# The second layer's values as two blocks of seven products, computed ahead of its pairs of heads

## The reference, cut to what matters

```python
h = jnp.einsum('bsd,de->bse', x, w_in[layer])            # 512 x 2048 times 2048 x 8192
qa, ka, va, ga, qb, kb, vb, gb = jnp.split(h, splits, axis=-1)   # eight of width 1024
ya = _dilated_attention(heads(qa, 16), heads(ka, 16), heads(va, 16), t5_bias)
yb = _neighbourhood_attention(heads(qb, 16), heads(kb, 16), heads(vb, 16), na_rpb[layer])
ya = merge(ya) * jax.nn.silu(ga.astype(jnp.float32))
yb = merge(yb) * jax.nn.silu(gb.astype(jnp.float32))
out = jnp.einsum('bse,ed->bsd', jnp.concatenate([ya, yb], -1), w_out[layer])
x = _layer_norm(DEEPNORM_ALPHA * x + out, ln_gain[layer], ln_bias[layer])
```

## Time and profile before

| | |
|---|---|
| median of three runs | 2478.79 us |
| the profiled execution, first to last instruction | 2477.0 us |
| PE busy | 2464.3 us (99%), 13712 matmuls |
| DVE busy | 1506.1 us (61%) |
| ACT busy | 841.0 us (34%) |
| POOL busy | 696.6 us (28%) |
| end of the first layer's products | about 1500 us |
| end of the pair steps | about 2310 us |

### The profile page before, as it was taken

The page is one execution under the profiler, slowest core; times in us unless marked ns, Lnnn a source line. Parts: engine busy times, 40 slices in busy tenths (PEclk is TensorE's granted clock), DMA queues, the critical chain, the costliest instruction groups (busy, mean ns, idle before and its releaser), DMA issues.

```text
span 2477.0 us, 36169 instructions
## 1 busy us (share of the span) xinstructions
PE 2464.3 (99%) x13712; PEld 2092.3 (84%) x13712; DVE 1506.1 (61%) x2529; ACT 841.0 (34%) x1281; POOL 696.6 (28%) x867
## 2 busy tenths in 40 slices
PE   9999999999999999999999999999999999999998
PEld 7788899999988888888888888888888888888887
DVE  5664877898779976655554333556465545455525
ACT  7422444544454333333222222223232322223221
POOL 0312455666512222232001220211122334343100
PEclk9999999999999999999999999999999999999999
DMA  7748333433456766777544444676656555546622
GB/s 287 223 162 271 114 126 128 130 135 136 137 173 211 259 230 237 241 244 274 178 165 149 136 153 128 205 196 205 205 176 212 172 175 160 171 153 214 242 96 102
DMA packets 102405, 452.53 MB, mean 183 GB/s; under 512 B 18006, under 2 KB 18006, under 8 KB 74182
## 3 DMA queue, kind: packets, MB, share of 16 engines
q1 hardware_dynamic: 38712, 241.58, 28.7%
q0 software_dynamic: 63568, 209.25, 26.8%
HBM read 351.47 MB, written 100.79 MB: 183 GB/s over the span
## 4 chain that ended last, share of the span: by engine, by line
PE 98%; DMA 1%; SPq 0%; DVE 0%; ACT 0%; issue 0%; DVEq 0%
PE bank L456 23%; PE bank L457 22%; PE bank L458 22%; PE bank L874 16%; PE bank L1258 5%; PE bank L1181 2%; PE bank L1319 2%; PE bank L1160 2%; PE bank L1043 1%; PE bank L1018 1%; DMA w_raw<-wst 1%; PE bank L955 1%; PE bank L1038 0%; PE bank L1008 0%; PE bank L898 0%; PE bank L713 0%
## 5 line engine op out<-in xcount | busy, mean ns | idle before, releaser
L445 DVE TENSOR_TENSOR w_lo<-w_raw,w_hi 128x2048 fp32r<-128x2048 f32 x164 | 375.9, 2292 | 369.5 <-ACT w_hi L440 367.3
L456 PE MATMUL bank<-act_b,w_hi 128*128 128x512 f32 x1280 | 501.6, 392 | 0.0
L457 PE MATMUL bank<-act_b,w_lo 128*128 128x512 f32 x1280 | 498.4, 389 | 0.0
L458 PE MATMUL bank<-act_b,w_hi 128*128 128x512 f32 x1280 | 498.1, 389 | 0.0
L440 ACT ACTIVATE w_hi<-w_raw 128x2048 fp32r<-128x2048 f32 x163 | 311.7, 1913 | 509.6 <-PE bank L458 435.9
L456 PE MATMUL bank<-act_a,w_hi 128*128 128x512 f32 (+1 forms) x1032 | 405.8, 393 | 0.0
L457 PE MATMUL bank<-act_a,w_lo 128*128 128x512 f32 (+1 forms) x1032 | 401.9, 389 | 0.0
L458 PE MATMUL bank<-act_a,w_hi 128*128 128x512 f32 (+1 forms) x1032 | 401.8, 389 | 0.0
L456 PEld LDWEIGHTS bank<-act_b,w_hi 128*128 128x128 f32 x1280 | 240.2, 188 | 54.5 <-issue 5.2
L458 PEld LDWEIGHTS bank<-act_b,w_hi 128*128 128x128 f32 x1280 | 240.3, 188 | 50.4
L457 PEld LDWEIGHTS bank<-act_b,w_lo 128*128 128x128 f32 x1280 | 240.3, 188 | 48.8
(11 more groups left out here) (376 smaller groups left out, 3351.7 us busy)
## 6 DMA issues: line engine op xcount, KB each, us to landing
w_raw<-wst SPq DMA_DIRECT2D x210, 1024.0 KB, 5.0
prob_t<-flip_d POOLq DMA_DIRECT2D x64, 512.0 KB, 4.8
flip_d<-flip POOLq DMA_DIRECT2D x56, 512.0 KB, 4.3
mix_d<-stage POOLq DMA_DIRECT2D x24, 512.0 KB, 3.2
mixg<-mix_d POOLq DMA_DIRECT2D x8, 1536.0 KB, 6.8
prob_tk<-flip_d POOLq DMA_DIRECT2D x32, 256.0 KB, 6.0
flip_d<-flip_a POOLq DMA_DIRECT2D x16, 512.0 KB, 2.9
b<-rows_2d POOLq DMA_DIRECT2D x16, 448.0 KB, 10.3
```

Source lines behind the costliest of these rows:

```text
L445: dve.tensor_tensor(w_lo[s][:], w_raw[s][:], w_hi[s][:].bitcast(F32), ALU.subtract).then_inc(lo_ready, 1)
L456: pe.matmul(out_ap, l_hi, r_hi, start=start, stop=False)
L457: pe.matmul(out_ap, l_lo, r_hi, start=False, stop=False)
L458: return pe.matmul(out_ap, l_hi, r_lo, start=False, stop=stop)
```

## The change

1. *Value stage.* Between the end of `wo_group` and pair step 0 stands a stage of 32 chunks (`value_chunk(n)`), which computes all 2048 value columns, token-major: tokens on the partitions, 512 columns in a bank. It consists of two blocks (`sg` 0 and 1, 1024 columns each). A block is a 2x2 split of tokens (256 each), inner dimension (1024 each) and columns (512 each), with seven products instead of eight (Strassen's scheme in Winograd's form): three in its first half (`ph` 0), four in its second, each over k = 0 to 7. The weights of a block are streamed in both halves, since four of the products use sums of weight blocks: chunks of 1536 columns in the first half and 2048 in the second.
2. *Sums of weights.* POOL makes them (`value_sums`), one per chunk in the first half and three in the second. ACT and DVE split each of the three or four parts on its own (`value_hi`, `value_lo`, 512 columns each). The sums have one buffer each, the split parts two.
3. *Sums of tokens.* Four sums of quarters of x1 are made once, from x1 in DRAM: all 16 tiles of x1 are now stored plainly to `x1_d` and loaded in quarters in the middle of the first half of block 0; two are DVE's (`s1_sum`, `s2_sum`), two POOL's (`s3_sum`, `s4_sum`), each in two pieces of 1024 columns, and each piece is split by ACT and DVE (`tokens_hi`, `tokens_lo`).
4. *Results.* DVE, ACT and POOL combine the seven products (`keep`, `first_block_out`, `u2_out` and so on), POOL stores them in 16 transfers per block to `v2_d`, which now holds all values.
5. *Pairs.* The pairs' weights hold queries, keys and gates only, cut as chunks of 1536, 1536, 1024 and 2048 columns (`PAIR_COLS`): 36, 36, 24 and 48 matmuls. Queries and keys are read after chunk 2, the gate after chunk 3, in a bank of its own (7). `v_to_tokens` is one load per dense pair (six per window pair). The 32 x 32 transposes and the four small stores go. On DVE the order in a beat changes: in beat 1 the split stands between `soft2_a` of tile 2 and of tile 3, and `queries_keys` between the flips. `beat` on PE is not changed.

The number of weight chunks goes from 216 to 248. The core of the diff:

```diff
+            def value_chunk(n):
+                sg, ph, k = v_phase(n)
+                operands = ((act_b, k, 0), (act_b, k + 8, 0), (s1_x, k, 0)) if ph == 0 else \
+                           ((s4_x, k, 0), (s3_x, k, 0), (s2_x, k, 0), (act_b, k + 8, 256))
+                order = V_ORDER[ph]
+                for pos, i in enumerate(order):
+                    if i + 1 < len(order):
+                        pe.wait_ge(vp_lo, VL0 + parts_before(n) + i + 1)
+                    else:
+                        pe.wait_ge(lo_ready, 2 * G_V + n + 1)
...
+                    act, row, c0 = operands[i]
+                    for t in range(2):
+                        for m, (l, r) in enumerate(((0, 0), (1, 0), (0, 1))):
+                            last = pe.matmul(v_bank(sg, ph, i, t), act[l][:, row, c0 + P * t:c0 + P * t + P], v_w[n % 2][i][r][:],
+                                             start=(k == 0 and m == 0), stop=(k == 7 and m == 2))
+                    last.then_inc(vp_used if pos + 1 < len(order) else chunk_used, 1)
```

```diff
+            def value_sums(n):
+                sg, ph, k = v_phase(n)
+                c = 2 * G_V + n
+                b11, b12, b21, b22 = (v_block(n, i) for i in range(4))
+                t1, t3, t2, t4 = v_sum
+                pool.wait_ge(w_loaded[n % 2], 8 * (c - n % 2) - 16)
+                jobs = ((t1, b12, b11, ALU.subtract),) if ph == 0 else \
+                       ((t3, b22, b12, ALU.subtract), (t2, t3[:], b11, ALU.add), (t4, t2[:], b21, ALU.subtract))
+                for i, (dst, l, r, op) in enumerate(jobs):
+                    if n:
+                        if ph == 0 or i == 2 or k == 0:
+                            pool.wait_ge(lo_ready, c)
+                        else:
+                            pool.wait_ge(vp_lo, VL0 + parts_before(n - 1) + i + 2)
...
+                    pool.tensor_tensor(dst[:], l, r, op).then_inc(vp_sum, 1)
```

```diff
+            # DVE, from chunk 3 to chunk 11 of the stage
+            value_lo(4, range(2))
+            s1_sum(1)
+            s2_sum(0)
+            tokens_lo(2, s1_x, s1_raw, 1)
+            value_lo(4, range(2, 3))
+            s2_sum(1)
+            value_lo(5)
+            tokens_lo(3, s3_x, s3_raw, 0)
+            value_lo(6)
+            tokens_lo(4, s2_x, s2_raw, 0, 2)
+            tokens_lo(5, s4_x, s4_raw, 0)
+            value_lo(7)
+            value_lo(8)
+            tokens_lo(6, s3_x, s3_raw, 1)
+            first_block_out(0)
```

```diff
             def pair_step(step, par, kind, before, gemm=True):
                 for cc in range(4):
                     if kind and cc % 2 == 0:
                         beat(kind, before, step, cc // 2, par)
...
-                    chunk_ready(pe, 2 * g + cc % 2)
-                    rows_t(pe, cc % 2, range(6), act_b, in2_banks(kind, cc))
...
+                    chunk_ready(pe, 4 * step + (2 * G_IN2 + cc))
+                    if cc < 3:
+                        for kt in range(PAIR_COLS[cc] // GC):
+                            k = 6 * cc + kt
+                            for n in range(2):
+                                last = mm3(pe, bank[n][:], wt(w_hi[cc % 2], kt, n * P, P), wt(w_lo[cc % 2], kt, n * P, P),
+                                           act_b[0][:, k, :], act_b[1][:, k, :], start=(k == 0), stop=(k == KT - 1))
```

More of the change, by code:

```diff
@@ new lines, in pair_step @@
+                    if cc < 3:
[5 more added lines that the diff above has]
+                    else:
+                        if not kind:
+                            pe.wait_ge(v_dve, VD0 + 20)
+                        else:
+                            pe.wait_ge(ev_act, evac_act(step - 1, 1))
+                            pe.wait_ge(ev_dve, evac_dve(step - 1, 1))
+                        for k in range(KT):
+                            last = mm3(pe, bank[GATE_BANK][:], wt(w_hi[1], k, 0, P, P), wt(w_lo[1], k, 0, P, P),
+                                       act_b[0][:, k, :], act_b[1][:, k, :], start=(k == 0), stop=(k == KT - 1))
+                            if k == CK - 1:
+                                last.then_inc(gate_half, 1)
@@ new lines, in _ @@
+            hi2(G_WO + 6)
+            x1_hi(3, 0)
+            split_hi(act, 2 * G_WO + 15, 1)
+            value_hi(0)
+            tokens_hi(s1_x, s1_raw, 0, 1, 0)
+            value_hi(1)
+            x1_hi(3, 1)
+            for n in range(2, 4):
+                value_hi(n)
+            value_hi(4, range(2))
+            tokens_hi(s1_x, s1_raw, 1, 2, 0)
+            value_hi(4, range(2, 3))
+            value_hi(5)
+            tokens_hi(s3_x, s3_raw, 0, 2, 1)
+            value_hi(6)
+            tokens_hi(s2_x, s2_raw, 0, 3, 1)
@@ L1704, in exp2 @@
+            keep(1, 1, v_p5, 2)
+            value_hi(25, range(2, 4))
+            for n in range(26, 32):
+                value_hi(n)
+            split_hi(act, 2 * G_IN2, 0, cols=PAIR_COLS[0])
             def exp2(kind, step, cc):
@@ new lines, in _ @@
+            split_lo(dve, 2 * G_WO + 15, 1)
+            value_lo(0)
+            s1_sum(0)
+            tokens_lo(1, s1_x, s1_raw, 0)
+            value_lo(1)
+            x1_out_of(3, 1, last=True)
+            for n in range(2, 4):
+                value_lo(n)
+            value_lo(4, range(2))
[6 more added lines that the diff above has]
+            tokens_lo(3, s3_x, s3_raw, 0)
@@ L2462, in soft2_a @@
+            value_lo(17)
+            third_block_out(0)
+            for n in range(18, 25):
+                value_lo(n)
+            first_block_out(1)
+            for n in range(25, 32):
+                value_lo(n)
+            split_lo(dve, 2 * G_IN2, 0, cols=PAIR_COLS[0])
+            u2_out(1)
+            u3_out(1)
+            second_block_out(1)
+            third_block_out(1)
             def soft2_a(kind, step, cc, par):
@@ new lines, in v_store @@
+            def v_store(src, row, col, done):
+                pool.wait_ge(*done)
+                for j in range(4):
+                    if col < 1024:
+                        at, step, block = 8 * row + j, 16, 4
+                    else:
+                        at, step, block = 256 * (j % 2) + 4 * row + j // 2, 8, 2
+                    pool.dma_start(bass.AP(v2_d, at * D + col, [[step * D, 32], [block * D, 2], [1, 512]]),
+                                   src[32 * j:32 * j + 32, :, :]).then_inc(v2_stored, 16)
@@ new lines, in _ @@
+            value_sums(2)
+            for s in range(2):
+                pool.wait_ge(x1_out[s], 464)
+            tokens_load(x_22, 12, 1, 1)
+            tokens_load(x_12, 12, 0, 3)
+            value_sums(3)
+            value_sums(4)
+            s3_sum(0)
+            value_sums(5)
+            s4_sum(0)
+            s3_sum(1)
+            value_sums(6)
+            s4_sum(1)
+            for n in range(7, 10):
+                value_sums(n)
+            v_store(v_u, 0, 0, (v_dve, VD0 + 2))
```

524 lines of the change are left out of this document (377 added, 147 removed).

## The result

The changed kernel takes 2540.3 us (median of 4 runs, 2539.2 to 2540.7) beside 2479.0 for the one before: 1.0249 times as long, 95% interval 1.0234 to 1.0264. The profiled execution's span is 2538.8 us. The forecast was slower, 2490 us, range 2463 to 2507: the sign is right, and the time lies outside the range.

The account below looks back on a forecast made before the run. TensorE's product count times their 0.227 us distance, plus its waits, was taken as the bound: 2477.0 - 21.8 + 31 (values' stage) + 2 (dense pairs) = 2488.2, plus 1.8 for the runs' median: 2490 us, range 2463 to 2507.

Parts of the forecast that it names:

- What bounds the kernel, and the 96 products: Whole kernel: TensorE's products, 0.227 us apart, set the time; 96 fewer products save 21.8 us.
- The values' stage, 31 us: New stage before the pairs: VectorE and GpSimd alternate on SBUF and stall TensorE by 31 us, bounds 0 to 45.
- 13, 8, 4 and 6: Values' stage: forecast stalls in us for first and second half of block one, then of block two.
- low parts read 1.7 us: Values' stage: sign that VectorE's 512-column low parts would read 1.7 us where GpSimd sums run.
- The dense pairs, 2 us with bounds 0 to 24: Dense pair steps: shorter half steps leave 0.8 us of cover for the second probabilities load, costing 2 us over 8 steps.
- load that is late by 2 us beside the bias loads: Dense steps: such a late load of flipped probabilities costs 1 to 2 us in a step.
- 0.7 us of work on DVE: Dense steps: queries and keys ahead of the last flip make it end some 0.7 us later.
- The landing of 21.7 against a need of 22.5: Dense steps: second probabilities load lands 21.7 us after the beat, its products come at 22.5, leaving 0.8 us.
- rival 2: Dense pairs lose 3 us each because loads land 25 us after the beat: +22, 2512 us; chance 0.10.
- Rival 1: Values' stage runs nearly at TensorE's pace: 2473 us, or 2457 with no stall; chance 0.30.
- Rival 3: Values' stage: sum and low part take two whole instructions, 1.96 us a pair: +15, 2505 us; chance 0.10.
- The windowed steps, 0: Window pairs use their flipped probabilities a step later, so they cost 0.

Follow-up runs that it names:

- Short sums: Changed kernel with GpSimd's weight-block sums made for 128 of 512 columns in all value-stage chunks but the first and ninth: span 2521.3 us, stage 170.1.
- sums on one engine: Changed kernel with all weight sums and the third and fourth kinds of token sums in the values' stage on VectorE instead of GpSimd: span 2512.1 us, stage 166.8.
- all mended and the weights held: Changed kernel with dense-step order, bias loads, VectorE sums, stage front, tail and token-load timing edited, plus held weight loads: 2471.5 us, ratio 0.9971 to the kernel before.
- keys last and biases early: Changed kernel with VectorE's queries and keys behind the second flip and bias loads ahead of the first flip's transfers: span 2503.2 us, half steps 324.5.
- the mended kernels: Changed kernel with dense-step, stage and tail edits combined: 2478.8 us; with token loads and sums later, 2480.6; with weight loads also held, 2471.5.

## Why the prediction was right or wrong

- **What bounds the kernel, and the 96 products:** right. The view of starts 0.227 us apart was the yardstick for all that followed.
- **The values' stage, 31 us:** nearly right in size (36.3) and right in mechanism. Measured loss by halves of blocks was 17.5, 6.7, 7.5 and 4.6 us against 13, 8, 4 and 6. Short sums, which leave the order as it is, took 18.8 us off, and sums on one engine 22.0, of which some 6 in the first half belong to POOL's order and its token sums. The signs named beforehand came (PE waiting for DVE's low parts from chunk 3 on, a stage of 189 us for 183 forecast), but "low parts read 1.7 us" did not: their starts are 1.70 apart, their records 1.55. Three terms were mis-sized. The first half came to 17.5 instead of 13: DVE is idle for 8.0 of its first 50 us, where 6 to 7 were put, and the rest is work over PE's pace, put at 6; no run separates the two further. The first half of block two came to 7.5 instead of 4: the twelve stores hold POOL from 1608.8 to 1615.2, 6.4 us where 7.8 were forecast, and DVE then idles 3.3 us with the sum late. And PE's slow clock behind stalls was left out: 18 of the stage's starts lie 0.43 us apart, 3.6 us over 0.227, and none does in that stretch before.
- **The dense pairs, 2 us with bounds 0 to 24:** this step failed; it is 40.4. The forecast costed the second load at 4.6 us, its median before, though single ones took up to 8.3, and kept the neighbours of before around it. It did write that the chunks are moved ("14 + 9 + 19 us", lengths that its rows don't give: at 0.227 us chunks of 36, 24 and 48 products are 8.2, 5.4 and 10.9), but used this for PE's work alone and not for the weights' requests. A split belongs to a chunk, and SyncE's weights follow the split: shorter chunks moved their request from 19 to 15.5 us behind the beat, while the flip, which follows the beat, stayed. Two transfers that had stood 2.9 us apart now run together, and the load takes up to 12.0 us. Holding the weights back gave 38.2 us back. The "load that is late by 2 us beside the bias loads" had named the wrong neighbour, and costed the lateness as a wait alone: the half clock behind the waits adds some 14 us to 25.4.
- **The same step, second error:** queries and keys ahead of the last flip were costed as 0.7 us of work on DVE. They are a wait for chunk 2, and so for every stall of PE, with the flip behind it (5.74 us idle, store at +19.6). That alone decides little: with the weights held, stores at +14.4 in the second halves cost under 2 us in all (seven first halves of 20.15 to 20.69 us where 20.07 is the least). With the crowded load it closes a loop, which is why moving this order alone gave 31.1 us. The landing of 21.7 against a need of 22.5 holds only for a kernel without the wait and without the weights beside the load: with all mended and the weights held it lands at +19.5 to +22.6. With keys last and biases early alone it still lands at +21.2 to +24.7, and 4.8 us of waits are left.
- **The rivals:** rival 2 (loads at 25 us after the beat, 3 us a pair, 2512) is what happened in kind: at the end of the first halves the load lands at +24.7 to +27.4 from the second step on, in the second halves at +24.8 to +29.9 behind the late store, and the loss is 5.1 us a pair, not 3. It was given 0.10 because the median load is 4.6 us; a median over steps of the old order was no evidence for the new one, and its own most, 8.3 us, already lay beyond the 5.4 us that 22.5 - 16.4 - 0.7 leave. Rival 1 (stage at pace) came only nearer, by other code: with the sums on DVE 14.3 us remain, with the rest mended 9.6. Rival 3 (the pair takes two whole instructions, 1.96 us), which followed the Trainium skill, "SBUF — State Buffer", section "Who interferes with whom", is out: starts lie 1.70 apart, as in the earlier trace rows. That an instruction of either engine waits for the other's, the trace shows again.
- **The tail, which the sum leaves out:** wrong by a few us. SyncE's first loads of y now wait for the eighth tile of the gate chunk, 5.4 us before the last step's end, and PE waits 4.0 us for the low half made from them. Starting the first load earlier took 0.9 us off.
- **The windowed steps, 0:** right. Between 2100 and 2200 PE is busy all 100.0 us.

What stays open: which part of the 5.3 us outside stage and dense steps is the tail's DVE queue and which the clock; and why the mended kernels' runs spread more than those of before. Nor is it shown how the two queues share the transfer engines; the runs show only that the load is slow beside the weights and not slow without them.

## What to carry to other kernels

When a loop is shortened, list every transfer with what triggers it: those triggered by the loop's beat and those triggered by its chunks move against each other, and a load's median from the old order says nothing once two that were staggered coincide. Look at what is issued within a load's flight, on every queue, and hold back the one with slack. In an in-order queue, cost an instruction by what it waits for and not by its length, and ask who stands behind it. Where two engines alternate on SBUF, try giving all of the work to the faster one.

## What the runs showed of the hardware

Two loads of 768 and 512 KB asked for 0.3 us apart, on SyncE's and GpSimd's queues, took 11.3 and 11.9 us; in the same half step with the larger one held back the smaller took 5.2. DVE and POOL side by side on SBUF need 1.70 us for a sum and a low part (starts 1.70 apart). DVE alone starts such instructions 0.60 us apart, 0.79 behind a sum that feeds the next one, so both take 1.2 to 1.4 us: here one engine is faster than two. After PE had idled 3.46 us its products ran at the 1.2 GHz level (0.43 us apart) until 1791.9, some 3.6 us. The same is seen behind waits of 2.2 and 2.4 us in the values' stage (at 1604.2 and 1640.7), and it adds to the price of such stalls.
